# Splitting the normalised rows in the mixer and loading both parts in the feed-forward

## The chip, the cores and the metric

The kernel runs on one core of a Trainium2 chip. The metric is the time of one execution on the device in microseconds, as the median of several runs.

## The reference, cut to what matters

One encoder layer for 2048 tokens of width 1024: a gated token mixer, a normalisation, and a feed-forward with a convolution over three tokens.

```
x    = x + mixed @ w_out                      # the mixer's output
h2   = rms_norm(x, norm2_g)                   # (2048, 1024)
up   = depthwise_conv_seq(h2 @ w_up, conv_w, conv_b)     # w_up: 1024 x 5632
val, gate = split(up, 2)
x    = x + (silu(gate) * val) @ w_down        # w_down: 2816 x 1024
out  = rms_norm(x, final_g)
```

The tensor h2 of this reference, transposed, is what the change is about; the kernel calls it hT.

## The kernel before, in words

**Precision.** TensorE takes operands of the type fp32r. To keep fp32 accuracy the kernel splits each operand into a head (the value rounded to fp32r) and a tail (the value less its head, again in fp32r), and makes three products of the four: head-head, head-tail, tail-head (the list SPLIT). Every matmul group of the large products therefore comes in threes. Normally ScalarE or VectorE copies to get the head, and VectorE or GpSimd subtracts to get the tail.

**Phases.** Five functions run one after the other, each in a block of its own that all engines enter and leave together: the input projections, the Fourier branch, the attention, `mixer_output_phase` (L992) and `conv_ffn_phase` (L1303). They hand data on through scratch tensors in device memory. The change touches the last two. Tiles of the mixer are named mo_... in the profile, those of the feed-forward ff_....

**The mixer.** There are 4 token blocks b of 512 tokens (NBLK, BLK), each of 4 token tiles t of 128 (TPB). A block first has 8 stages s (L1257): 24 matmuls with the weight tile mix(s), which give 128 channels of both branches; VectorE gates and adds them (`gated`), and ScalarE and VectorE split the sum (`mix_heads`, `mix_tails`). Then each token tile is multiplied by w_out (`output`, L1272) in two halves of 24 matmuls. VectorE adds the residual half by half and normalises (`finish`), with ScalarE's `stats` between; TensorE transposes the normalised tile in 8 pieces of 128x128 into PSUM (`turn`, L1282); ScalarE copies these with the gain norm2_g as its scale into mo_turned and stores them to hT (`spill`, L1225 and L1228). `turn` and `spill` of a token tile n come one tile later; those of a block's last tile come at stage s = 1 of the next block, and the very last behind everything.

Each engine executes its own list strictly in order. In the mixer's stages the weights come through two raw buffers: SP loads a weight tile when the tail of the tile two before it is made, VectorE makes the head (`w_heads`, L1142), GpSimd the tail (`w_tails`, L1102), and TensorE waits for the tail. In the list of VectorE the call `w_heads(b, s, 2)` makes the heads of mix(s + 1) and out(s) ahead of `gated(b, s)`. In the output part VectorE also makes the heads of the next block's activations (`a_heads`, L1148), two for each token tile, and GpSimd their tails (L1107).

**The feed-forward.** The buffer h holds head and tail of the whole hT in SBUF. For each of 44 output tiles of 128 channels (`up`, L1644) TensorE runs 4 token blocks of 24 matmuls each, ScalarE takes out the result with the middle tap of the convolution (L1585), VectorE adds the side taps (L1490, L1493), and after each pair the product of both is stored. The second half of the phase multiplies by w_down (L1664).

At the start of the phase SP loads the weight tile 0, the 8 row blocks of hT of token block 0 into the 8 places of hraw, a small table, weight tile 1, and then the 24 row blocks of token blocks 1 to 3, each when its place in hraw is free (L1380). ScalarE makes the head of each (L1575), VectorE the tails of k = 0 to 5 (L1484) and GpSimd those of k = 6 and 7 (L1453). TensorE's tile 0 waits for the tail of each k of each block on its own.

Of the kernel before, what the change touches and what calls it, by code (L numbers as in the profile page):

```python
# [992 lines left out]
def mixer_output_phase(nc, x, fnT, atT, gT, w_mix, w_out, norm_g, eye, x2_out, hT_out):  # L993
# [7 lines left out]
    with ExitStack() as ctx:  # L1001
# [12 lines left out]
        turned_sb = m.sb("turned", [P, 1, KD, P])  # L1014
# [14 lines left out]
        turned, evac = m.sem("turned_mm"), m.sem("evac")  # L1029
# [91 lines left out]
        def _(dve):  # L1121
# [62 lines left out]

            w_heads(0, 0, 1)
            for k in range(KA):
                a_heads(0, k)
            for b in range(NBLK):
                for s in range(KD):
                    w_heads(b, s, 2 if s < KD - 1 or b < NBLK - 1 else 1)  # L1190
                    gated(b, s)
                    if s:
                        mix_tails(b * KD + s - 1)
                mix_tails(b * KD + KD - 1)
                for t in range(TPB):
                    finish(b, t)
                    if b < NBLK - 1:
                        a_heads(b + 1, 2 * t)
                        a_heads(b + 1, 2 * t + 1)

        @block.scalar
        def _(act):
# [40 lines left out]
            act.wait_ge(hT_stored, 16 * NTOK)  # L1243

        @block.tensor
        def _(pe):
# [52 lines left out]
def conv_ffn_phase(nc, x2, hT, w_up, w_down, conv, final_g, hid_d, out):  # L1299
# [6 lines left out]
    RING, RAW, HRAW = 3, 2, 8  # L1306
# [6 lines left out]
    with ExitStack() as ctx:  # L1313
# [7 lines left out]
        with ExitStack() as first:  # L1321
            hraw = Pool(nc, first, "ff").sb("hraw", [P, HRAW, BLK])
# [3 lines left out]
        with ExitStack() as first:  # L1326
# [9 lines left out]
        h_in, h_head, h_tail_dve, h_tail_pool = (  # L1336
            m.sems("h_in", HRAW), m.sem("h_head"), m.sem("h_tail_dve"), m.sem("h_tail_pool"))
# [10 lines left out]
        POOL_TAILS = (6, 7)  # L1348
        DVE_TAILS = tuple(k for k in range(KD) if k not in POOL_TAILS)

# [5 lines left out]

        def wait_h_tail(engine, b, k):
            if k in POOL_TAILS:
                engine.wait_ge(h_tail_pool, len(POOL_TAILS) * b + POOL_TAILS.index(k) + 1)
            else:  # L1360
                engine.wait_ge(h_tail_dve, len(DVE_TAILS) * b + DVE_TAILS.index(k) + 1)

# [3 lines left out]
        def _(sp):  # L1366
# [374 lines left out]
```

## Time and profile before

| | |
|---|---|
| runs | 3146.33 us median of 3 (3138.73 to 3149.79) |
| profiled execution | 3149.32 us, its span 3147.4 us |
| TensorE (PE) busy | 91% of the span |
| VectorE (DVE), ScalarE (ACT), GpSimd (POOL) busy | 38%, 22%, 22% |
| DMA | 349.22 MB, 111 GB/s over the span |
| mixer_output_phase | about 1180 to 1642 us |
| conv_ffn_phase, its start | first load at 1641.92 us |

In the rows below, times are in microseconds from the start of the span unless marked ns. A row of the timeline begins with the start and the duration of a run of like instructions; then come the engine, the line of the kernel, the operation, the destination and the sources with their shapes, the number of instructions, and in brackets the idle time of the engine before them and what ended it. PEld is TensorE's loading of weights, SPq and ACTq are the DMA issues of these engines. A row of the windows gives a stretch, its length, busy time and number of instructions of each engine, then the clock granted to TensorE as a share of full speed, the mean busy share of the 16 DMA engines, and what they moved.

### The profile page before, as it was taken

To read this page: it belongs to the slowest core of one execution; us is meant where nothing else is said; L and a number is where in the kernel's file an instruction comes from. 1 tells how busy PE (TensorE), PEld (TensorE's weight loads), DVE (VectorE), ACT (ScalarE), POOL (GpSimd) and SP (SyncE) were. 2 spreads that over 40 slices of the span, in tenths; PEclk is the share of its full clock that TensorE was granted. 3 is DMA by queue.
4 is the path that set the end of the run, shared out by engine and by line. 5 is a ranking of instruction groups with operands and counts; after the bars stand their busy time and mean duration, and the time that the engine had idled before them with its cause. 6 is when DMAs were issued, how large, how long until landed. Compare 5 with 4: busy or idle time off the path is not lost. (4 is left out here: it accounts for less than half of the span.)

```text
span 3147.4 us, 33077 instructions
## 1 busy us (share of the span) xinstructions
PE 2873.8 (91%) x13320; PEld 2361.9 (75%) x13320; DVE 1209.0 (38%) x1656; ACT 677.6 (22%) x1254; POOL 703.6 (22%) x293
## 2 busy tenths in 40 slices
PE   7999999993549996998879999999999998999998
PEld 6888888883548884776767888888888887888886
DVE  5200000004549885456534232323232323464564
ACT  4211111111236650211123111111111111111011
POOL 1010101012112315345412001100110011444442
PEclk9999999997769998999989999999999999999999
DMA  4321212113286736566643101110111013554543
GB/s 142 92 85 68 69 68 77 67 70 116 74 182 162 185 92 201 189 199 194 200 139 130 54 27 54 54 54 27 54 54 54 31 51 123 178 196 151 197 171 107
DMA packets 179704, 349.22 MB, mean 111 GB/s; under 512 B 59253, under 2 KB 80497, under 8 KB 173425
## 3 DMA queue, kind: packets, MB, share of 16 engines
q1 hardware_dynamic: 160624, 330.55, 32.9%
q10 hardware_dynamic: 18944, 16.78, 1.6%
q8 instruction: 95, 1.56, 0.2%
q14 instruction: 41, 0.33, 0.0%
HBM read 257.03 MB, written 91.78 MB: 111 GB/s over the span
## 5 line engine op out<-in xcount | busy, mean ns | idle before, releaser
L1644 PE MATMUL ff_psum<-ff_h,ff_w 128*128 128x512 f32 x4224 | 988.6, 395 | 17.7 <-DVE ff_h L1484 16.6
L1644 PEld LDWEIGHTS ff_psum<-ff_h,ff_w 128*128 128x128 f32 x4224 | 791.2, 187 | 215.1 <-POOL ff_w L1446 14.9
L1446 POOL TENSOR_TENSOR ff_w<-ff_wraw,ff_w 128x1024 fp32r<-128x1024 f32 x132 | 318.6, 2414 | 1190.3 <-DVE ff_w L1478 1190.3
L357 PE MATMUL in_psum<-in_hT,in_w 128*128 128x512 f32 x2304 | 522.6, 389 | 0.0
L357 PEld LDWEIGHTS in_psum<-in_hT,in_w 128*128 128x128 f32 x2304 | 432.6, 188 | 89.6
L1664 PE MATMUL ff_psum<-ff_w,ff_hid 128*128 128x512 f32 x2112 | 481.6, 391 | 9.3 <-DVE ff_hid L1502 9.1
L1664 PEld LDWEIGHTS ff_psum<-ff_w,ff_hid 128*128 128x128 f32 x2112 | 397.9, 188 | 92.9 <-issue 10.1
L1257 PE MATMUL mo_psum<-mo_act,mo_w 128*128 128x512 f32 x768 | 196.4, 412 | 59.4 <-POOL mo_w L1102 37.9
L1257 PEld LDWEIGHTS mo_psum<-mo_act,mo_w 128*128 128x128 f32 x768 | 147.9, 197 | 105.6 <-POOL mo_w L1102 47.9
L202 POOL TENSOR_TENSOR in_w<-in_wraw,in_w 128x1024 fp32r<-128x1024 f32 x32 | 77.1, 2413 | 620.4 <-DVE in_w L279 310.7
L1490 DVE SCALAR_TENSOR_TENSOR ff_gate<-ff_psum,ff_param,ff_gate 128x2047 f32<-128x2047 f32 x22 | 51.7, 2350 | 372.9 <-ACT ff_gate L1585 372.9
L348 PE MATMUL in_psum<-in_w,in_hT 128*128 128x512 f32 x768 | 180.9, 395 | 4.8 <-DVE in_hT L249 4.8
L1272 PE MATMUL mo_psum<-mo_wo,mo_mixed 128*128 128x512 f32 x768 | 178.2, 392 | 5.3 <-DVE mo_mixed L1164 5.3
L1478 DVE CAST ff_w<-ff_wraw 128x1024 fp32r<-128x1024 f32 x132 | 96.3, 730 | 217.6 <-PE ff_psum L1664 178.7
L348 PEld LDWEIGHTS in_psum<-in_w,in_hT 128*128 128x128 f32 x768 | 144.9, 190 | 35.0 <-DVE in_hT L249 5.2
L1272 PEld LDWEIGHTS mo_psum<-mo_wo,mo_mixed 128*128 128x128 f32 x768 | 143.2, 188 | 36.4 <-DVE mo_mixed L1164 7.3
L1585 ACT ACTIVATE ff_gate<-ff_psum,ff_param 128x512 f32<-128x512 f32 x88 | 68.5, 778 | 422.6 <-PE ff_psum L1644 422.6
L1490 DVE SCALAR_TENSOR_TENSOR ff_val<-ff_psum,ff_param,ff_val 128x2047 f32<-128x2047 f32 x22 | 51.7, 2350 | 271.5 <-ACT ff_val L1585 271.5
L1502 DVE TENSOR_TENSOR ff_hid<-ff_kraw,ff_hid 128x1024 fp32r<-128x1024 f32 x44 | 128.8, 2928 | 21.2 <-ACT ff_hid L1595 21.1
L960 PE MATMUL at_psum<-at_vs,at_pT 128*128 128x64 f32 x1024 | 134.5, 277 | 0.0
L276 DVE COPY in_bias_now<-in_gbias 128x1 f32 x16 | 2.5, 153 | 335.6 <-ACT in_stage L335 292.9
L960 PEld LDWEIGHTS at_psum<-at_vs,at_pT 128*128 128x128 f32 x1024 | 130.9, 201 | 0.0
(119 smaller groups left out, 2393.5 us busy)
## 6 DMA issues: line engine op xcount, KB each, us to landing
ff_wraw<-in_w_down_dram SPq DMA_DIRECT2D x88, 512.0 KB, 3.3
ff_wraw<-in_w_up_dram SPq DMA_DIRECT2D x44, 512.0 KB, 5.8
hidden<-ff_val SPq DMA_DIRECT2D x22, 1024.0 KB, 4.9
ff_kraw<-hidden SPq DMA_DIRECT2D x44, 512.0 KB, 4.5
at_bias<-shifted SPq DMA_DIRECT2D x72, 256.0 KB
in_wraw<-in_w_in_dram SPq DMA_DIRECT2D x32, 512.0 KB, 3.7
gT<-in_stage SPq DMA_DIRECT2D x64, 256.0 KB, 2.4
mo_wraw<-in_w_mix_dram SPq DMA_DIRECT2D x32, 512.0 KB, 3.8
```

Of the source, the lines that this page charges most:

```text
L202: nc.gpsimd.tensor_tensor(w[:, 1, s], wraw[:, t % RAW], f32(w[:, 0, s]), ALU.subtract).then_inc(w_tail, 1)
L348: last = nc.tensor.matmul(ps[:, bank(n)], hT[:, a, k, t * P:(t + 1) * P], w[:, b, 0:4, k], start=(k == 0 and (a, b) == SPLIT[0]), stop=(k ...
L357: last = nc.tensor.matmul(ps[:, bank], w[:, a, s, k], hT[:, c, k, b * BLK:(b + 1) * BLK], start=(k == 0 and (a, c) == SPLIT[0]), stop=(k = ...
L960: last = nc.tensor.matmul(ps[:, OB[n % 2], 0:HEAD_DIM], pT[:, n % 3, k], vs[:, h % 2, (ROW0[i] // 4 + k) * TJ + j], start=(k == 0), stop=( ...
L1257: last = nc.tensor.matmul(ps[:, 2 * (n % 2) + branch], w[:, a, s % 2, k], act_s[:, c, k], start=(k == ks[0] and (a, c) == SPLIT[0]), stop= ...
L1272: last = nc.tensor.matmul(ps[:, 4 + half], mixed[:, a, k, t * P:(t + 1) * P], wo[:, c, k, half * SPH:(half + 1) * SPH], start=(k == 0 and ...
L1446: nc.gpsimd.tensor_tensor(w[:, 1, n % RING], wraw[:, n % RAW], f32(w[:, 0, n % RING]), ALU.subtract).then_inc(w_tail, 1)
L1478: V.tensor_copy(w[:, 0, n % RING], wraw[:, n % RAW]).then_inc(w_head, 1)
L1490: V.scalar_tensor_tensor(out=dst[:, 1:SEQ], in0=row[:, 0:SEQ - 1], scalar=param[:, t, 0:1], in1=dst[:, 1:SEQ], op0=ALU.mult, op1=ALU.add). ...
L1502: V.tensor_tensor(hid[:, 1, n % 2], kraw[:, :, :], f32(hid[:, 0, n % 2]), ALU.subtract).then_inc(k_tail, 1)
L1644: last = nc.tensor.matmul(ps[:, 4 * (t % 2) + b], w[:, a, t % RING, k * P:(k + 1) * P], h[:, c, k, b * BLK:(b + 1) * BLK], start=(k == 0 a ...
L1664: last = nc.tensor.matmul(ps[:, 4 * half + i], hid[:, a, (b * PAIRS + pair) % 2, q, i * P:(i + 1) * P], w[:, c, n % RING, q * HALF:(q + 1) ...
```

## The change

In the mixer VectorE makes the tails of the transposed tile, too: PSUM value times gain, less the head. The tile mo_turned holds both parts. `spill` waits for the eight tails and stores both parts to hT, which gets a leading dimension of 2. In the feed-forward SP loads heads and tails straight to their places in h, with 64 loads of 256 KB in place of 32; hraw and the splitting of h go. The first token block waits for each k's two loads, the others for all 16 of their block. TensorE's `turn` waits for the tails where it waited for the heads.

```diff
@@ mixer_output_phase
-        turned_sb = m.sb("turned", [P, 1, KD, P])
+        turned_sb = m.sb("turned", [P, 2, KD, P], F32R)
@@ vector
+            def h_tails(n):
+                for k in range(KD):
+                    dve.wait_ge(h_head, KD * n + 4 * (k // 4) + 4)
+                    V.scalar_tensor_tensor(out=turned_sb[:, 1, k], in0=ps[:, 6 + k // 4, (k % 4) * P:(k % 4 + 1) * P],
+                                           scalar=gain[:, k:k + 1], in1=f32(turned_sb[:, 0, k]),
+                                           op0=ALU.mult, op1=ALU.subtract).then_inc(h_tail, 1)
...
                     gated(b, s)
                     if s:
                         mix_tails(b * KD + s - 1)
+                    if b and s == 1:
+                        h_tails(b * TPB - 1)
                 mix_tails(b * KD + KD - 1)
                 for t in range(TPB):
                     finish(b, t)
+                    if t:
+                        h_tails(b * TPB + t - 1)
                     if b < NBLK - 1:
                         a_heads(b + 1, 2 * t)
                         a_heads(b + 1, 2 * t + 1)
+            h_tails(NTOK - 1)
@@ scalar
             def spill(n):
                 act.wait_ge(turned, n + 1)
                 if n:
-                    act.wait_ge(hT_stored, 16 * n)
+                    act.wait_ge(hT_stored, 32 * n)
                 for k in range(KD):
                     nc.scalar.activation(turned_sb[:, 0, k], ps[:, 6 + k // 4, (k % 4) * P:(k % 4 + 1) * P], ACT.Copy,
-                                         scale=gain[:, k:k + 1]).then_inc(evac, 1)
-                act.wait_ge(evac, KD * (n + 1))
-                act.dma_start(hT_out.rearrange("(k p) t -> p k t", p=P)[:, :, n * P:(n + 1) * P],
-                              turned_sb[:, 0]).then_inc(hT_stored, 16)
+                                         scale=gain[:, k:k + 1]).then_inc(h_head, 1)
+                act.wait_ge(h_tail, KD * (n + 1))
+                for part in range(2):
+                    act.dma_start(hT_out[part].rearrange("(k p) t -> p k t", p=P)[:, :, n * P:(n + 1) * P],
+                                  f32(turned_sb[:, part])).then_inc(hT_stored, 16)
@@ tensor
             def turn(n):
                 pe.wait_ge(h2_done, n + 1)
-                at_least(pe, evac, KD * n)
+                at_least(pe, h_tail, KD * n)
@@ conv_ffn_phase, sync
             def load_h(b, k):
-                n = b * KD + k
-                if n >= HRAW:
-                    wait_h_tail(sp, b - 1, k)
-                sp.dma_start(hraw[:, k], hT[k * P:(k + 1) * P, b * BLK:(b + 1) * BLK]).then_inc(h_in[k], 16)
+                for part in range(2):
+                    sp.dma_start(f32(h[:, part, k, b * BLK:(b + 1) * BLK]),
+                                 hT[part, k * P:(k + 1) * P, b * BLK:(b + 1) * BLK]).then_inc(h_in[b + KD - 1 if b else k], 16)
@@ gpsimd, vector, scalar: h_tails and h_heads and the waits for them are gone
-            w_tails(0)
-            h_tails(0)
-            h_tails(1)
-            h_tails(2)
-            w_tails(1)
-            h_tails(3)
-            for n in range(2, TILES):
+            for n in range(TILES):
                 w_tails(n)
...
             w_heads(0)
-            for b in range(NBLK):
-                h_tails(b)
-                if b == 2:
-                    w_heads(1)
+            w_heads(1)
...
-            for b in range(NBLK):
-                for k in range(KD):
-                    h_heads(b, k)
             act.wait_ge(const_in, 16)
-            act.wait_ge(h_tail_pool, len(POOL_TAILS) * NBLK)
-            act.wait_ge(h_tail_dve, len(DVE_TAILS) * NBLK)
@@ tensor
                         if t == 0:
-                            wait_h_tail(pe, b, k)
+                            pe.wait_ge(h_in[b + KD - 1 if b else k], 32 * (KD if b else 1))
@@ encoder_layer
-    x2, hT = scratch("x2", SEQ, D), scratch("hT", D, SEQ)
+    x2, hT = scratch("x2", SEQ, D), scratch("hT", 2, D, SEQ)
```

## Rows read from the trace of the kernel before

**Rows 1.** Page, part 1: busy us, share of the span, instructions.

```profile
PE 2873.8 (91%) x13320; PEld 2361.9 (75%) x13320; DVE 1209.0 (38%) x1656; ACT 677.6 (22%) x1254; POOL 703.6 (22%) x293
```

**Rows 2.** Windows at the feed-forward's start, and one in the mixer's stages.

```profile
core 0: us, PE busy (x) PEld busy (x) DVE busy (x) ACT busy (x) POOL busy (x), PEclk, DMA share, GB/s
1642.00:1646.00 4.00, 0.00 (x0) 0.00 (x0) 0.50 (x1) 0.00 (x0) 0.00 (x0) 0.50 0.73 212
1646.00:1674.00 28.00, 21.99 (x84) 16.28 (x85) 20.82 (x26) 20.22 (x32) 13.90 (x9) 0.89 0.98 339
1650.00:1658.00 8.00, 8.00 (x31) 6.10 (x30) 4.54 (x8) 5.41 (x9) 2.58 (x2) 0.87 1.04 388
1644.00:1648.00 4.00, 0.00 (x0) 0.00 (x0) 0.69 (x1) 0.63 (x1) 1.73 (x1) 0.50 0.99 279
...
1556.00:1560.00 4.00, 4.00 (x12) 3.13 (x11) 3.97 (x5) 0.63 (x1) 2.38 (x1) 0.57 0.51 153
```

**Rows 3.** Timeline of the feed-forward's start.

```profile
1641.92 0.33 SPq L1374 DMA_DIRECT2D ff_wraw<-in_w_up_dram  x1
...
1646.27 2.34 POOL L1446 TENSOR_TENSOR ff_w<-ff_wraw,ff_w 128x1024 fp32r<-128x1024 f32 x1 [61.55 <-DVE ff_w L1478]
...
1649.31 11.53 PE L1644 MATMUL ff_psum<-ff_h,ff_w 128*128 128x512 f32 x42 [14.53 <-DVE ff_h L1484]
...
1673.22 0.63 ACT L1575 ACTIVATE ff_h<-ff_hraw 128x512 fp32r<-128x512 f32 x1 [0.15 <-DMA ff_hraw<-hT]
...
1675.54 44.83 PE L1644 MATMUL ff_psum<-ff_h,ff_w 128*128 128x512 f32 x191 [0.45 <-DVE ff_h L1484]
```

**Rows 4.** VectorE's groups by form: busy us, mean ns of one, idle before.

```profile
L583 DVE TENSOR_TENSOR ft_X<-ft_psum,ft_X 128x512 fp32r<-128x512 f32 x16 | 10.5, 686 | 11.7 <-ACT ft_X L628 11.7
...
L583 DVE TENSOR_TENSOR ft_X<-ft_psum,ft_X 128x256 fp32r<-128x256 f32 x4 | 1.7, 414 | 0.0
...
L594 DVE SCALAR_TENSOR_TENSOR ft_out<-ft_psum,ft_real 128x128 f32<-128x128 f32 x4 | 1.5, 380 | 0.0
```

**Rows 5.** Timeline from the end of mixer block 1 into block 2.

```profile
1418.10 2.15 ACT L1225 ACTIVATE mo_turned<-mo_psum,mo_gain 128x128 f32<-128x128 f32 x8
...
1419.11 0.75 DVE L1183 TENSOR_SCALAR mo_h<-mo_xt,mo_rstd 128x1024 f32<-128x1024 f32 x1
1419.78 0.76 DVE L1148 CAST mo_act<-mo_araw 128x512 fp32r<-128x512 f32 x2
...
1420.28 3.07 POOL L1107 TENSOR_TENSOR mo_act<-mo_araw,mo_act 128x512 fp32r<-128x512 f32 x2 [9.15 <-DVE mo_act L1148]
...
1423.31 2.81 POOL L1102 TENSOR_TENSOR mo_w<-mo_wraw,mo_w 128x1024 fp32r<-128x1024 f32 x1
...
1426.17 7.36 PE L1257 MATMUL mo_psum<-mo_act,mo_w 128*128 128x512 f32 x24 [1.80 <-POOL mo_w L1102]
...
1435.98 0.68 DVE L1164 TENSOR_TENSOR mo_mixed<-mo_mix,mo_mixed 128x512 fp32r<-128x512 f32 x1
...
1436.63 2.15 ACT L1225 ACTIVATE mo_turned<-mo_psum,mo_gain 128x128 f32<-128x128 f32 x8
1436.66 0.70 DVE L1142 CAST mo_w<-mo_wraw 128x1024 fp32r<-128x1024 f32 x1
...
1439.88 5.31 PEld L1257 LDWEIGHTS mo_psum<-mo_act,mo_w 128*128 128x128 f32 x24 [0.42 <-POOL mo_w L1102]
```

**Rows 6.** Timeline of the mixer's last token tiles.

```profile
1631.56 0.75 DVE L1183 TENSOR_SCALAR mo_h<-mo_xt,mo_rstd 128x1024 f32<-128x1024 f32 x1
1632.72 0.38 ACTq L1228 DMA_DIRECT2D hT<-mo_turned  x1
...
1636.01 2.17 ACT L1225 ACTIVATE mo_turned<-mo_psum,mo_gain 128x128 f32<-128x128 f32 x8 [3.32 <-DMA hT<-mo_turned]
1638.21 0.38 ACTq L1228 DMA_DIRECT2D hT<-mo_turned  x1
```

**Rows 7.** DMA view, 1632 to 1642 us: GB/s in 40 slices of 0.25 us.

```profile
GB/s 0 0 0 0 0 0 92 297 285 293 293 295 289 246 8 0 0 0 0 0 33 0 0 0 0 0 0 0 102 303 291 293 287 287 293 236 6 0 0 0
```

More of the change, by code:

```diff
@@ L1028, in mixer_output_phase @@
             m.sem(s) for s in ("out_mm", "x2_done", "sumsq_done", "mean_done", "root_done", "h2_done"))
-        turned, evac = m.sem("turned_mm"), m.sem("evac")
+        turned, h_head, h_tail = m.sem("turned_mm"), m.sem("h_head"), m.sem("h_tail")
         x2_stored, hT_stored = m.sems("x2_stored", 3), m.sem("hT_stored")
@@ L1242, in _ @@
                 act.wait_ge(x2_stored[s], 16 * len(range(s, NTOK, 3)))
-            act.wait_ge(hT_stored, 16 * NTOK)
+            act.wait_ge(hT_stored, 32 * NTOK)
         @block.tensor
@@ L1305, in conv_ffn_phase @@
     TILES = UP + NBLK * DOWN
-    RING, RAW, HRAW = 3, 2, 8
+    RING, RAW = 3, 2
     HALF = D // 2
@@ L1320, in conv_ffn_phase @@
         val0 = m.sb("val0", [P, SEQ])
-        with ExitStack() as first:
-            hraw = Pool(nc, first, "ff").sb("hraw", [P, HRAW, BLK])
         val1 = m.sb("val1", [P, SEQ])
@@ L1335, in conv_ffn_phase @@
         const_in, gain_in = m.sem("const_in"), m.sem("gain_in")
-        h_in, h_head, h_tail_dve, h_tail_pool = (
-            m.sems("h_in", HRAW), m.sem("h_head"), m.sem("h_tail_dve"), m.sem("h_tail_pool"))
+        h_in = m.sems("h_in", KD + NBLK - 1)
         w_in, w_head, w_tail, used = m.sems("w_in", RAW), m.sem("w_head"), m.sem("w_tail"), m.sem("used")
@@ L1345, in conv_ffn_phase @@
             m.sem(s) for s in ("added", "sumsq_done", "mean_done", "root_done", "step", "y_done", "stored"))
-        POOL_TAILS = (6, 7)
-        DVE_TAILS = tuple(k for k in range(KD) if k not in POOL_TAILS)
         def tile_done(engine, n):
@@ L1355, in tile_done @@
                 engine.wait_ge(up_mm, NBLK * (n + 1))
[L1357 to L1361, printed above, removed]
         block = ctx.enter_context(nc.Block())
@@ L1447, in w_tails @@
                                         ALU.subtract).then_inc(w_tail, 1)
-            def h_tails(b):
-                for k in POOL_TAILS:
-                    pool.wait_ge(h_head, b * KD + k + 1)
-                    at = slice(b * BLK, (b + 1) * BLK)
-                    nc.gpsimd.tensor_tensor(h[:, 1, k, at], hraw[:, k], f32(h[:, 0, k, at]),
-                                            ALU.subtract).then_inc(h_tail_pool, 1)
-            w_tails(0)
-            h_tails(0)
-            h_tails(1)
-            h_tails(2)
-            w_tails(1)
-            h_tails(3)
-            for n in range(2, TILES):
+            for n in range(TILES):
                 w_tails(n)
@@ L1478, in w_heads @@
                 V.tensor_copy(w[:, 0, n % RING], wraw[:, n % RAW]).then_inc(w_head, 1)
-            def h_tails(b):
-                for k in DVE_TAILS:
-                    dve.wait_ge(h_head, b * KD + k + 1)
-                    at = slice(b * BLK, (b + 1) * BLK)
-                    V.tensor_tensor(h[:, 1, k, at], hraw[:, k], f32(h[:, 0, k, at]), ALU.subtract).then_inc(h_tail_dve, 1)
             def sides(t):
@@ L1571, in _ @@
         def _(act):
-            def h_heads(b, k):
-                n = b * KD + k
-                act.wait_ge(h_in[k], 16 * (b + 1))
-                nc.scalar.activation(h[:, 0, k, b * BLK:(b + 1) * BLK], hraw[:, k], ACT.Copy).then_inc(h_head, 1)
             def centre(t, b):
```

## Prediction

> **What bounds the kernel now.** I read the page first, then the slices of the trace around the two functions that the change touches. TensorE is busy 2873.8 us of a span of 3147.4 [rows 1], so a change counts where TensorE stands still, or where it makes TensorE stand still. There are three such places: the start of the feed-forward, the seam between the functions, and the starts of the mixer's token blocks.
>
> At the start of the feed-forward the reader is to see the DMA engines, not ScalarE or VectorE. From 1646 to 1674 their busy share is 0.98 and they move 339 GB/s; in the best 8 us of it 388, in the 4 us around its start 279 [rows 2]. In that time the 32 raw blocks of hT arrive (8.39 MB), with weight tiles. The first matmul starts at 1649.31, when the first weight tile has its tail (GpSimd from 1646.27, 2.34 us), the last block has landed by 1673.22, where ScalarE takes it up, and from 1675.54 TensorE runs 191 matmuls in 44.83 us, 0.235 us each, without a stop [rows 3]. Nine of these belong to output tile 0 (96 matmuls in all, 87 came before, the first 42 of them in the row at 1649.31), so tile 0 ends at 1675.54 + 9 x 0.235 = 1677.7. The conversion in the feed-forward is therefore covered by a transfer that already fills the engines. After it TensorE is bound by itself.
>
> **The feed-forward's start, part by part.** Removed: 32 ScalarE copies, 24 VectorE and 8 GpSimd subtractions. Their cover was the transfer, so their removal is worth nothing but the lag from last landing to last matmul. Added: the loads are now 64 x 256 KB, 16.78 MB. Before the last one come weight tiles 0 and 1 and the table param (1.14 MB), 17.92 MB together; 4 us at 212 GB/s are 0.85 MB by 1646 [rows 2]. The other 17.07 MB take 50.4 us at 339 GB/s, so the last block lands at 1696.4 on the old time axis, 23.2 us later than 1673.2. Bounds: 44.0 us at 388 GB/s, 61.2 us at 279, so 16.8 to 34.0 us later. I take 339, the rate of the longest stretch of the same loads. SP's issues are not the limit: there are 32 more of about 0.5 us, 33 us in all for 64, beside 50.
>
> Blocks 1 to 3 each wait for all 16 of their pieces. So after the last landing all 24 matmuls of block 3 remain, 24 x 0.235 = 5.6 us, where before 1677.7 - 1673.2 = 4.5 us remained: 1.1 us more. TensorE also stands still about half of the time before: 4.19 MB at 339 GB/s are 12.4 us for a block with 5.6 us of matmuls. The clock falls after gaps: in 1556 to 1560, behind a gap at the weights, it was granted 0.57 and 12 matmuls ran in place of 17 [rows 2], 5 x 0.235 = 1.2 us. I put 1.5 us for block 3, between none and 5.6 us (all of it at 1.2 GHz in place of 2.4). Together **D = 23.2 + 1.1 + 1.5 = 25.8 us** (17.9 to 40.7). That SP asks for tile 2's weights only behind all 64 loads costs nothing: tile 1 was asked for before most of them and gives 22.5 us of matmuls. Late next is nothing that I see: the shift of tile 0 is the shift of the phase.
>
> The Trainium skill, "DMA: Bandwidth & Descriptors", § Bandwidth, gives 425 GB/s for a 16 MB load by one core alone and near 358 GB/s as a core's share of the memory. By 425 the 17.07 MB would take an estimated 40.2 us and D would be 15.6; by 358, 47.7 us and 23.1. The same page, § Issuing engines are not separate DMA queues, says that queues share the 16 engines, so neither splitting the issues nor moving them would help. The trace's 0.98 share at 339 speaks for the second figure, and the sum does not use either.
>
> **The tails in the mixer.** Added: 128 VectorE instructions of 128x128 from PSUM, eight for each of 16 token tiles. None such is in the trace. Nearest: a subtraction from PSUM of 512 columns takes 686 ns, of 256 columns 414, so 128 columns should take 278; a scalar_tensor_tensor of 128x128 from PSUM took 380 [rows 4]. I take 0.28 us, since the slope of the latter group (another line, with another output pattern) is steeper throughout: 8 x 0.28 = 2.2, with the switch-over 2.3 us a tile (up to 3.0). By the Trainium skill's "VectorE: DVE Perf Modes", § The TRN2 errata, an fp32 tensor_tensor takes (N + 151)/0.96 ns, an estimated 0.29 us here, which would change the sum by under 1 us.
>
> Twelve of the sixteen groups of tails stand right behind finish. Eight of these (t = 1 and 2) cost nothing: VectorE next waits for a 5.6 us half of output matmuls, and TensorE needs that half's sum only one half later. The one at t = 3 of block 3 belongs to the seam, below. At t = 3 of blocks 0 to 2 the next stage's start hangs on VectorE. In block 2: h2 is ready at 1419.87, the casts of the last two activations follow at once (1419.78 on the merged row), GpSimd makes their tails from 1420.28 to 1423.35 and then the weight tail of stage 1 from 1423.31, and TensorE, idle, starts stage 1 at 1426.17, as that ends [rows 5]. The tails of tile 4b+2 go between h2 and the casts; their heads are ready (ScalarE 1418.10 + 2.15). The chain moves by 2.3 us, and SP's next weight load, which waits for that tail, with it. **A = 3 x 2.3 = 6.9 us** (up to 9.1).
>
> The other three seams are at s = 1. VectorE ends mix_tails at 1436.66 and casts the weights of stage 3 at once; TensorE starts that stage behind their tail at 1439.88 [rows 5]. Now VectorE first does the tails of the last token tile of the block before. ScalarE makes their heads only from 1436.63, in 2.15 us; the first four tails start at about 1437.8 and end at 1438.9, the other four end at 1440.1. What queues behind them on VectorE is the cast, behind that GpSimd's tail, TensorE's stage 3 and SP's next load: 1440.1 - 1436.7 = 3.4 us. The load - cast - tail loop runs slower than TensorE to the end of the stages (the same loop lets TensorE stand still in most of them), so I let the delay stay. **B = 3 x 3.4 = 10.2 us** (up to 12.5).
>
> ScalarE's wait for the tails holds up stats(n+1) only, which comes some 9 us later. TensorE's wait for them in turn comes a token tile later. Both are covered, except at the end.
>
> **The seam.** Tile 15's h2 ends at 1632.31; the store of tile 14 was issued at 1632.72, landed by 1636.01, where ScalarE takes up the heads of tile 15, whose store goes out at 1638.21, and the feed-forward's first load at 1641.92, all of it one chain with TensorE idle [rows 3, 6]. Now the tails of tile 14 stand behind h2: 1632.31 + 2.24 = 1634.55, 1.8 us later than 1632.72. Two stores follow in place of one. A store of 0.52 MB moves at about 290 GB/s [rows 7], so the second adds 1.8 us to the landing. Behind the last heads come the last four tails, 4 x 0.28 + 0.1 = 1.2 us, and then again two stores, 1.8. **C = 1.8 + 1.8 + 1.2 + 1.8 = 6.6 us** (3.8 if a second store costs only its 0.38 us issue, 7.8 with tails of 0.38).
>
> **The sum.** A + B + C + D = 6.9 + 10.2 + 6.6 + 25.8 = 49.5 us on the profiled execution of 3149.3 us: 3198.8. The median of the runs is 3.0 us below that execution: **3195.8**.
>
> **Rivals.** First, the mixer's stages absorb the delays: if the load - cast - tail loop has slack, or VectorE catches up before stage 7, A and B vanish, and 3195.8 - 17.1 = 3178.7 is left. For it: the loop for the out weights waits mostly for DMAs. Against: TensorE starts stage 3 within 0.2 us of being free, behind a weight tail.
>
> Second, the doubled stream runs at its slowest rate, 279 GB/s, with TensorE's last block at 1.2 GHz: D = 40.7, and 3210.7. For it: the first 4 us of the loads ran so. Against: the 24 us after them were faster, with three engines at work on the same memory.
>
> Third, not slower: the start of the feed-forward hides the doubled transfer. Tile 0 took 28.4 us (1649.3 to 1677.7) for 22.5 us of matmuls, so 5.9 us could be won if conversion were what it waits for; with A and B absorbed and C = 6.6 the result would be 3147. It decides at the rate: the last block must land by 1672, which is 17.07 MB in 26 us, 657 GB/s. The trace's best is 388.
>
> **Chances.** Forecast 0.60, first rival 0.20, second 0.15, third 0.03, and 0.02 for a gain that I don't see. The range reaches from below the first rival to above the second: 3173 to 3213. A difference under 0.3% (9 us) can hardly be told from none: faster 0.01, same 0.03, slower 0.96.
>
> **What would show it.** In the profile after: (D) a DMA share near 1 for some 50 us from the feed-forward's start, three gaps of about 6 us in TensorE, and the uninterrupted run starting 25 us later in relation to the first matmul; (A, B) stage 1 of blocks 1 to 3 some 2.3 us later behind the last transpose, stage 3 a further 3.4; (C) some 6.6 us more from the last output matmul to the first load. It is wrong if the loads run over 400 GB/s or under 280, if the tails take over 0.4 us each, or if TensorE's idle time in the stages doesn't grow.

## The result, and the profile after

The changed kernel is slower: 3192.32 us median of 4 runs (3190.47 to 3196.40), against 3144.22 us for the kernel before in the same series, a ratio of 1.0155 with a 95% interval from 1.0133 to 1.0176. A second series on another occasion gave 3189.50 against 3147.02 us, 1.0144 (1.0127 to 1.0161); two slow runs of the kernel before in that series (3236.62 and 4553.74 us, at granted clocks of 0.883 and 0.600) are left out of the ratio. The prediction was 3195.8 us, 49.5 us over before; measured were 48.1 and 42.5 us.

The page of the profiled execution, parts 1 and 3 (for DMA queues: packets, megabytes, share of 16 engines):

```profile
span 3188.7 us, 33188 instructions
...
PE 2885.1 (90%) x13320; PEld 2373.9 (74%) x13320; DVE 1217.6 (38%) x1760; ACT 659.2 (21%) x1222; POOL 692.0 (22%) x285
...
q10 hardware_dynamic: 35584, 25.17, 2.5%
```

TensorE's work is what it was [rows 1]; VectorE has 104 instructions more (128 tails added, 24 removed). The whole moved 366.01 MB in place of 349.22: one more store of hT (q10 is ScalarE's queue) and one more load. Two executions also differ by chance: the mixer's first transpose came at 1281.38 us here and at 1285.19 before, 3.8 us earlier, for code that the change does not touch. So I read distances within each trace and not positions.

**The feed-forward's start.** Windows of the changed kernel, columns as in rows 2:

```profile
1664.00:1713.00 49.00, 26.35 (x74) 18.76 (x75) 1.39 (x2) 2.33 (x3) 4.68 (x2) 0.71 1.02 370
...
1684.00:1692.00 8.00, 1.13 (x3) 0.94 (x4) 0.00 (x0) 0.00 (x0) 0.00 (x0) 0.50 1.05 376
1692.00:1700.00 8.00, 7.10 (x23) 5.26 (x21) 0.00 (x0) 0.78 (x1) 0.00 (x0) 0.74 1.05 389
```

and its timeline, to be held against rows 3:

```profile
1660.15 0.33 SPq L1375 DMA_DIRECT2D ff_wraw<-in_w_up_dram  x1
...
1667.41 5.32 PE L1612 MATMUL ff_psum<-ff_h,ff_w 128*128 128x512 f32 x12 [19.26 <-POOL ff_w L1446]
1672.96 0.96 PE L1612 MATMUL ff_psum<-ff_h,ff_w 128*128 128x512 f32 x3 [0.24 <-DMA ff_h<-hT]
1675.81 3.93 PE L1612 MATMUL ff_psum<-ff_h,ff_w 128*128 128x512 f32 x9 [1.88 <-DMA ff_h<-hT]
1690.87 8.23 PE L1612 MATMUL ff_psum<-ff_h,ff_w 128*128 128x512 f32 x24 [11.13 <-DMA ff_h<-hT]
1701.69 7.39 PE L1612 MATMUL ff_psum<-ff_h,ff_w 128*128 128x512 f32 x24 [2.59 <-DMA ff_h<-hT]
1712.48 12.78 PE L1612 MATMUL ff_psum<-ff_h,ff_w 128*128 128x512 f32 x47 [3.40 <-DMA ff_h<-hT]
...
1719.93 0.78 ACT L1558 ACTIVATE ff_val<-ff_psum,ff_param 128x512 f32<-128x512 f32 x1 [10.03 <-PE ff_psum L1612]
```

The DMA engines are busy throughout (share 1.02) while VectorE, ScalarE and GpSimd do next to nothing. TensorE waits for the pieces of every block and runs the 24 matmuls of each of blocks 1 to 3 in 7.3 to 8.2 us in place of 5.6, at a lower clock behind the gaps (granted 0.50 in the row from 1684, most of which is a gap, and 0.71 over the stretch). The last block's wait ends 1712.48 - 1660.15 = 52.3 us behind the first load. ScalarE takes up tile 0's last sum at 59.8 us, and TensorE has begun tile 1 at 59.6; before, it did so at 35.8 (1677.7 - 1641.92). That is 23.8 us more. (The expectations below say 24.0, from 59.8 less 35.8, which are two different marks.)

**The seam.** Timeline of the changed kernel, to be held against rows 6:

```profile
1643.23 0.75 DVE L1183 TENSOR_SCALAR mo_h<-mo_xt,mo_rstd 128x1024 f32<-128x1024 f32 x1
1643.90 2.15 DVE L1188 SCALAR_TENSOR_TENSOR mo_turned<-mo_psum,mo_gain,mo_turned 128x128 fp32r<-128x128 f32 x8
1646.09 1.00 ACTq L1241 DMA_DIRECT2D hT<-mo_turned  x2
...
1651.23 2.17 ACT L1237 ACTIVATE mo_turned<-mo_psum,mo_gain 128x128 fp32r<-128x128 f32 x8 [6.61 <-DMA hT<-mo_turned]
1652.40 2.16 DVE L1188 SCALAR_TENSOR_TENSOR mo_turned<-mo_psum,mo_gain,mo_turned 128x128 fp32r<-128x128 f32 x8 [6.35 <-ACT mo_turned L1237]
1654.60 1.00 ACTq L1241 DMA_DIRECT2D hT<-mo_turned  x2
```

Four steps grew, each against its own in rows 6 and 3: from the end of h2 to the store of tile 14 2.1 us in place of 0.4; that store to the next heads 5.1 in place of 3.3; those heads to the store of tile 15 3.4 in place of 2.2; that store to the first load 5.6 in place of 3.7. Together 1.7 + 1.8 + 1.2 + 1.8 = 6.5 us.

**The mixer's blocks.** TensorE at the start of block 2 in the changed kernel (transposes are the 128x128 rows):

```profile
1416.79 1.03 PE L1295 MATMUL mo_psum<-mo_ident,mo_h 128*128 128x128 f32 x8
1417.58 4.34 PE L1270 MATMUL mo_psum<-mo_act,mo_w 128*128 128x512 f32 x18
1426.09 2.88 PE L1270 MATMUL mo_psum<-mo_act,mo_w 128*128 128x512 f32 x6 [4.17 <-POOL mo_act L1107]
1429.64 7.46 PE L1270 MATMUL mo_psum<-mo_act,mo_w 128*128 128x512 f32 x24 [0.67 <-POOL mo_w L1102]
1436.94 1.04 PE L1295 MATMUL mo_psum<-mo_ident,mo_h 128*128 128x128 f32 x8
1437.73 5.73 PE L1270 MATMUL mo_psum<-mo_act,mo_w 128*128 128x512 f32 x24
1446.95 12.80 PE L1270 MATMUL mo_psum<-mo_act,mo_w 128*128 128x512 f32 x48 [3.49 <-POOL mo_w L1102]
```

The same place in the kernel before, where the last row holds stages 2 and 3:

```profile
1415.69 1.03 PE L1282 MATMUL mo_psum<-mo_ident,mo_h 128*128 128x128 f32 x8
...
1434.15 11.46 PE L1257 MATMUL mo_psum<-mo_act,mo_w 128*128 128x512 f32 x48
```

Stage 1 starts 12.85 us behind the transpose at 1416.79; before, it was 1426.17 [rows 5] behind the transpose at 1415.69, 10.48 us. Stage 3 starts 9.2 us behind stage 2 (1446.95 less 1437.73) in place of 5.7 (1439.88 less 1434.15). What stands in between on VectorE and GpSimd:

```profile
1440.18 2.15 ACT L1237 ACTIVATE mo_turned<-mo_psum,mo_gain 128x128 fp32r<-128x128 f32 x8
1441.33 2.16 DVE L1188 SCALAR_TENSOR_TENSOR mo_turned<-mo_psum,mo_gain,mo_turned 128x128 fp32r<-128x128 f32 x8 [1.13 <-ACT mo_turned L1237]
1443.41 0.69 DVE L1142 CAST mo_w<-mo_wraw 128x1024 fp32r<-128x1024 f32 x1
...
1444.17 2.72 POOL L1102 TENSOR_TENSOR mo_w<-mo_wraw,mo_w 128x1024 fp32r<-128x1024 f32 x1 [5.12 <-DVE mo_w L1142]
```

The tails wait for their heads, the cast of stage 3's weights waits for the tails, and GpSimd for the cast: the chain of the prediction. A measure for all three blocks is the time from the mixer's first transpose to its last but one. The first two rows are the kernel before, the last two the changed one:

```profile
1285.19 1.03 PE L1282 MATMUL mo_psum<-mo_ident,mo_h 128*128 128x128 f32 x8
...
1628.14 1.03 PE L1282 MATMUL mo_psum<-mo_ident,mo_h 128*128 128x128 f32 x8
```

```profile
1281.38 1.04 PE L1295 MATMUL mo_psum<-mo_ident,mo_h 128*128 128x128 f32 x8
...
1639.82 1.03 PE L1295 MATMUL mo_psum<-mo_ident,mo_h 128*128 128x128 f32 x8
```

342.9 us and 358.4 us, 15.5 us more. With 6.5 and 23.8 that makes 45.8 us, between the two measured differences.

The windows of just these stretches say in what form TensorE spends the 15.5 us (before, then changed):

```profile
1285.19:1628.14 342.95, 309.79 (x1361) 248.27 (x1360) 184.11 (x277) 63.01 (x178) 144.83 (x69) 0.98 0.58 186
```

```profile
1281.38:1639.82 358.44, 317.75 (x1362) 254.79 (x1360) 209.67 (x389) 63.07 (x178) 146.70 (x69) 0.95 0.62 198
```

It idles 40.7 us in place of 33.2, and it is at work 317.7 us in place of 309.8 on the same matmuls, at a granted clock of 0.95 in place of 0.98. Over the four profiled executions with the mixer of before, idle is 31.2 to 34.7 and work 309.0 to 313.3; over the five with the changed mixer they are 40.7 to 44.0 and 313.1 to 317.7. So the waits are the larger part on average, and behind them the matmuls run slower: stage 3 of blocks 1 and 3 took 8.55 us in place of 5.73. How much of this a later wait would have filled anyway is not shown.

Three distances, in us, will do for all kernels below. "Blocks" is the one just read, "seam" goes from the last transpose but one to the feed-forward's first load, "start" from there to ScalarE's first take-out of output tile 1 (which follows tile 0 by its first block). Where the code of a stretch is the same, "blocks" differs by up to 1.9 us from one execution to another (342.9 to 344.8 with the mixer of before), "start" by up to 1.7 (41.6 to 43.3 with the feed-forward of before), "seam" by 0.1.

| kernel | blocks | seam | start | ratio to before (95% interval) |
|---|---|---|---|---|
| before | 342.9 | 13.8 | 41.6 | |
| changed | 358.4 | 20.3 | 65.4 | 1.0155 (1.0133 to 1.0176) |
| changed, again | 358.2 | 20.4 | 65.6 | 1.0144 (1.0127 to 1.0161) |
| mixer's part alone | 357.8 | 20.4 | 41.6 | 1.0058 (1.0045 to 1.0072) |
| feed-forward's part alone | 344.6 | 13.8 | 66.1 | 1.0067 (1.0054 to 1.0080) |
| one part loaded, no splitting | 344.8 | 13.8 | 43.1 | 1.0000 (0.9991 to 1.0008) |
| stores alone | 347.3 | 17.8 | 43.3 | 1.0017 (1.0006 to 1.0027) |
| tails alone | 358.0 | 16.6 | 42.2 | 1.0046 (1.0033 to 1.0059) |
| changed, tails moved | 354.1 | 20.4 | 65.3 | 1.0110 (1.0096 to 1.0125) |
| changed, early store | 356.9 | 17.8 | 63.9 | 1.0134 (1.0116 to 1.0153) |
| changed, two tiles | 358.2 | 20.4 | see below | 1.0091 (1.0074 to 1.0107) |
| changed, finer waits | 357.0 | 20.4 | 59.4 | 1.0114 (1.0098 to 1.0131) |
| changed, all four | 349.2 | 17.8 | see below | 1.0039 (1.0026 to 1.0052) |
| before, two tiles | 343.6 | 13.8 | see below | 0.9983 (0.9974 to 0.9991) |

### The profile page after: what moved, and what is told of

Same layout as the page of the kernel before. It is cut to its first block and busy times, and to the rows that moved or that the text cites. A ratio compares the mean times of both kernels' runs of the same rounds, so it can differ in the third digit from the quotient of the medians.

```text
span 3188.7 us, 33188 instructions
## 1 busy us (share of the span) xinstructions
PE 2885.1 (90%) x13320; PEld 2373.9 (74%) x13320; DVE 1217.6 (38%) x1760; ACT 659.2 (21%) x1222; POOL 692.0 (22%) x285
## 2 busy tenths in 40 slices
DMA packets 200952, 366.01 MB, mean 115 GB/s; under 512 B 60020, under 2 KB 97648, under 8 KB 194672
## 5 line engine op out<-in xcount | busy, mean ns | idle before, releaser
L1612 PEld LDWEIGHTS ff_psum<-ff_h,ff_w 128*128 128x128 f32 x4224 | 800.9, 190 | 234.0 <-DMA ff_h<-hT 22.8
L1270 PE MATMUL mo_psum<-mo_act,mo_w 128*128 128x512 f32 x768 | 204.2, 426 | 67.8 <-POOL mo_w L1102 38.2
L1270 PEld LDWEIGHTS mo_psum<-mo_act,mo_w 128*128 128x128 f32 x768 | 154.5, 206 | 115.3 <-POOL mo_w L1102 47.9
L348 PEld LDWEIGHTS in_psum<-in_w,in_hT 128*128 128x128 f32 x768 | 144.5, 190 | 34.7 <-DVE in_hT L249 5.2
L1558 ACT ACTIVATE ff_val<-ff_psum,ff_param 128x512 f32<-128x512 f32 x88 | 68.1, 773 | 330.5 <-PE ff_psum L1612 330.5
```

Source lines behind the costliest of these rows:

```text
L348: last = nc.tensor.matmul(ps[:, bank(n)], hT[:, a, k, t * P:(t + 1) * P], w[:, b, 0:4, k], start=(k == 0 and (a, b) == SPLIT[0]), stop=(k ...
L1270: last = nc.tensor.matmul(ps[:, 2 * (n % 2) + branch], w[:, a, s % 2, k], act_s[:, c, k], start=(k == ks[0] and (a, c) == SPLIT[0]), stop= ...
L1558: nc.scalar.activation(dst[:, b * BLK:(b + 1) * BLK], ps[:, 4 * (t % 2) + b], ACT.Identity, scale=param[:, t, 1:2], bias=param[:, t, 3:4]) ...
L1612: last = nc.tensor.matmul(ps[:, 4 * (t % 2) + b], w[:, a, t % RING, k * P:(k + 1) * P], h[:, c, k, b * BLK:(b + 1) * BLK], start=(k == 0 a ...
```

## The experiments

**Each half alone.** The first kernel has the changed mixer and the feed-forward of before:

```diff
-                sp.dma_start(hraw[:, k], hT[k * P:(k + 1) * P, b * BLK:(b + 1) * BLK]).then_inc(h_in[k], 16)
+                sp.dma_start(hraw[:, k], hT[0, k * P:(k + 1) * P, b * BLK:(b + 1) * BLK]).then_inc(h_in[k], 16)
```

> The mixer of the changed kernel with the feed-forward of before: the mixer makes and stores both parts, the feed-forward loads the first part as its raw rows and splits them, so the tails of hT are left out of the products. Measures A + B + C alone. The theory of the prediction: about 22 us over before (17 in the mixer's blocks 1 to 3, 6.6 at the seam); read from the trace of the changed kernel 15.5 + 6.6 = 22. Rival (the delays in the stages are an accident of one execution, or come from the doubled transfer behind them): under 10 us. The distance from the last transpose but one to the feed-forward's first load: 20.3 us here, 13.8 before. From that load on the phase is as before.

The second has the mixer of before and the changed feed-forward:

```diff
-                                 hT[part, k * P:(k + 1) * P, b * BLK:(b + 1) * BLK]).then_inc(h_in[b + KD - 1 if b else k], 16)
+                                 hT[k * P:(k + 1) * P, b * BLK:(b + 1) * BLK]).then_inc(h_in[b + KD - 1 if b else k], 16)
```

> The mixer of before with the feed-forward of the changed kernel: both parts are loaded from the raw rows, so the second part holds the rows again in place of their tails. Measures D alone, the doubled transfer without the splitting. The theory: 24 us over before (24.0 in the changed kernel's trace from the first load to the last sum of output tile 0), mixer and seam as before. If A to D are independent, the two halves add up to the whole, 46 to 48 us. Rival (the start of the feed-forward suffers from the mixer's later end, its clock or its stores in flight): D alone well under 24.

Measured: 1.0058 and 1.0067. By the ratios that is 18 and 21 us, by the medians 22.0 and 22.4 (3169.43 and 3169.90 against 3147.47). Each half shows its own distances and leaves the others as before: 357.8 and 20.4 with a start of 41.6; 344.6 and 13.8 with a start of 66.1. The halves together give 39 us by the ratios, where the whole, measured twice, gives 49 and 45; by the medians 44.4, against 48.1 and 42.5. By the trace the halves add up (14.9 + 6.6 + 24.5 = 46.0), so I take them as independent; with intervals of some 4 us to either side on each half and 5 to 7 on the whole, the runs don't speak against it, and nothing that only both together cost shows in a row.

**What the removed splitting was worth.** The feed-forward half again, with one part in place of two:

```diff
-                for part in range(2):
+                for part in range(1):
                     sp.dma_start(f32(h[:, part, k, b * BLK:(b + 1) * BLK]),
...
-                                                    h[:, c, k, b * BLK:(b + 1) * BLK],
+                                                    h[:, 0, k, b * BLK:(b + 1) * BLK],
```

> As the one before, with one part loaded in place of two (8.39 MB as in the kernel before, but straight into place and without splitting); the matmuls read the first part in place of the second, so the tails of hT are left out of the products, their number is the same. Measures what the removed splitting is worth alone. The theory (the transfer binds, the splitting was covered): the last block lands as before, some 31 us after the first load, then 24 matmuls: tile 0 ends 1 to 3 us later than before, the whole is within 3 us of before. Rival (conversion was what tile 0 waited for): 5.9 us faster than before. Against the run with both parts: some 22 us less, which is 8.39 MB at 370 GB/s, if bytes set the time.

Measured 1.0000: the 64 instructions that the change takes off three engines are worth nothing that can be measured. The start is 1.5 us later, no more than it varies with the feed-forward of before. Both parts against one: 66.1 - 43.1 = 23.0 us for 8.39 MB, 365 GB/s. The trace adds a point that I had not put so:

```profile
1648.18 8.11 PE L1599 MATMUL ff_psum<-ff_h,ff_w 128*128 128x512 f32 x24 [15.08 <-POOL ff_w L1433]
1659.86 100.50 PE L1599 MATMUL ff_psum<-ff_h,ff_w 128*128 128x512 f32 x423 [3.57 <-DMA ff_h<-hT]
```

With one part TensorE waits once, 3.57 us for block 1, and never again. One part keeps up with TensorE from there (2.1 MB per 5.6 us of matmuls are 375 GB/s, about what the engines move), two parts cannot. The kernel before, which loads as many bytes, stands near this edge too.

**More work for each block.** If D is TensorE waiting with too little to do, another order helps:

```diff
-            for t in range(UP):
-                up(t)
+            for b in range(NBLK):
+                up(0, [b])
+                up(1, [b])
+            for t in range(2, UP):
+                up(t, range(NBLK))
```

> The changed kernel with another order of TensorE's first two output tiles in the feed-forward: block by block, each for tile 0 and tile 1, in place of tile by tile. All eight banks of PSUM are in use for it as before. Each block now brings 11.2 us of matmuls for some 11.3 us of its transfer. The theory (D is a transfer that TensorE waits for with too little work at hand): the end of tiles 0 and 1 moves from 82.3 us behind the first load (59.8 + 22.5) to about 52.3 + 11.3 + 1 = 65 us, 17 us less than the changed kernel, and the clock no longer falls between the blocks. Rival (D comes from the traffic itself, as slower matmuls, weights or stores): under 5 us of gain.

```profile
1651.94 0.33 SPq L1377 DMA_DIRECT2D ff_wraw<-in_w_up_dram  x1
...
1670.98 1.64 PE L1614 MATMUL ff_psum<-ff_h,ff_w 128*128 128x512 f32 x3 [1.92 <-DMA ff_h<-hT]
1675.70 64.52 PE L1614 MATMUL ff_psum<-ff_h,ff_w 128*128 128x512 f32 x263 [3.08 <-POOL ff_w L1448]
```

From 1675.70 TensorE runs without a stop. 168 of the 192 matmuls of both tiles remain there and take 42.1 us (39.4 at full clock; granted were 0.81 in the first 14 us and 0.93 over the whole), so tile 2 starts 65.9 us behind the first load, in place of 82.0 in the changed kernel. That is 16 us less. In the runs: 1.0091 against 1.0144, 17 us by the ratios and 16 by the medians, as expected, though the engines still move 369 GB/s at a share of 1.03 in the 48 us from 1656. So the cost was TensorE waiting with too little to do, not the traffic as such. What stops TensorE last is now the tail of weight tile 1 (3.08 us, GpSimd).

**Finer waits.** Blocks 1 to 3 wait for pairs of k:

```diff
-                            pe.wait_ge(h_in[b + KD - 1 if b else k], 32 * (KD if b else 1))
+                            pe.wait_ge(h_in[KD + 4 * (b - 1) + k // 2 if b else k], 32 * (2 if b else 1))
```

> The changed kernel with finer waits in the feed-forward: blocks 1 to 3 wait for each pair of k on its own (four semaphores a block) in place of all 16 pieces. The theory: after the last landing only 6 of 24 matmuls remain, and TensorE works a little all the time; tile 0 ends 2 to 3 us behind the last landing in place of 7.4, so 4 to 5 us less than the changed kernel. Rival (the coarse waits cost nothing, since the clock and not the count of matmuls sets the lag): under 2 us.

The start is 59.4 us in place of 65.4, and the ratio 1.0114 in place of 1.0144, an interval that overlaps (1.0098 to 1.0131 against 1.0127 to 1.0161) with the middle 9 us lower; the medians are 6 us apart. The rows show how:

```profile
1707.01 1.67 PE L1612 MATMUL ff_psum<-ff_h,ff_w 128*128 128x512 f32 x6 [1.05 <-DMA ff_h<-hT]
1709.68 30.60 PE L1612 MATMUL ff_psum<-ff_h,ff_w 128*128 128x512 f32 x130 [1.00 <-DMA ff_h<-hT]
```

A pair comes each 2.7 us (1.05 MB, 388 GB/s), with 1.66 us of matmuls and a gap of 1.05 us, and in gaps so short the clock stayed up (granted 1.00 from 1685 to 1713): six matmuls take 1.66 us, where 24 behind a gap of 11.1 us took 8.2. The start is 6.0 us earlier, so of the lag of 7.3 us behind the last landing about 6 were the coarse wait and its clock.

**The seam.** The first part is stored before the tails are made:

```diff
-                act.wait_ge(h_tail, KD * (n + 1))
-                for part in range(2):
+                for part, ready in enumerate((h_head, h_tail)):
+                    act.wait_ge(ready, KD * (n + 1))
```

> The changed kernel, but spill stores the first part as soon as the heads are made and waits for the tails only then, for the second part. The theory of the seam (C = waits for tails, then two stores one behind the other, twice): the first store moves while the tails are made, the second one's landing then hangs on the tails and one store's 3.3 us: some 1.7 us less at the store of tile 14 and 1.2 at that of tile 15. From the last transpose but one to the first load 17.4 us in place of 20.3 (13.8 before); in total 2.9 us less than the changed kernel. Rival (each issue on ScalarE or the landing costs a fixed time, not the queueing of the bytes): no change.

The seam is 17.8 us in place of 20.3, 2.6 less where 2.9 were expected. The ratio, 1.0134 against 1.0144, can't show so little. Blocks and start came out 1.5 us shorter each, within what they vary by.

**Moving the tails.** Here an expectation failed:

```diff
                     w_heads(b, s, 2 if s < KD - 1 or b < NBLK - 1 else 1)
+                    if b and s == 0:
+                        h_tails(b * TPB - 2)
+                    if b and s == 2:
+                        h_tails(b * TPB - 1)
                     gated(b, s)
...
-                    if b and s == 1:
-                        h_tails(b * TPB - 1)
...
-                    if t:
+                    if t and (t < TPB - 1 or b == NBLK - 1):
                         h_tails(b * TPB + t - 1)
```

> The changed kernel with two of the calls for tails moved in VectorE's list: those of a block's third tile from ahead of the casts of the last activations to behind the weight casts of stage 0, those of its last tile from stage 1 to behind the weight casts of stage 2. Nothing else differs. The theory (VectorE's order makes A and B): stage 1 of blocks 1 to 3 again 10.5 us behind the last transpose (12.9 in the changed kernel), stage 3 again 5.7 to 7.3 us behind stage 2 (9.2 to 10.9), and some 15 us less than the changed kernel, so some 31 to 33 us over before. Rival (the doubled stores delay the weights, whatever the order): no change in those distances and 46 to 48 us over before.

```profile
1300.33 1.03 PE L1297 MATMUL mo_psum<-mo_ident,mo_h 128*128 128x128 f32 x8
...
1310.79 7.68 PE L1272 MATMUL mo_psum<-mo_act,mo_w 128*128 128x512 f32 x24 [1.19 <-POOL mo_w L1102]
...
1319.11 5.73 PE L1272 MATMUL mo_psum<-mo_act,mo_w 128*128 128x512 f32 x24
1326.37 5.73 PE L1272 MATMUL mo_psum<-mo_act,mo_w 128*128 128x512 f32 x24 [1.54 <-POOL mo_w L1102]
1334.54 7.37 PE L1272 MATMUL mo_psum<-mo_act,mo_w 128*128 128x512 f32 x24 [2.43 <-POOL mo_w L1102]
```

Both marks are back: stage 1 stands 10.46 us behind the transpose, stage 3 7.3 us behind stage 2. But the blocks took 354.1 us, only 4.3 less than changed, not 15. Stage 2 now comes 8.3 us behind stage 1 (6.5 before), stage 4 8.2 behind stage 3 (7.7 before), stage 5 8.4 behind stage 4 (7.2 before): the delay moved on. The runs, 1.0110 or 35 us over before, look nearer to the 31 to 33 expected, but the three distances add up to 41.4 us over before; in the profiled execution the mixer's first transpose came 8.4 us earlier than before, in code that the change doesn't touch. I go by the distances. Two kernels took the cause apart. One stores twice and makes no tails:

```diff
-                for k in range(KD):
-                    dve.wait_ge(h_head, KD * n + 4 * (k // 4) + 4)
-                    V.scalar_tensor_tensor(out=turned_sb[:, 1, k], in0=ps[:, 6 + k // 4, (k % 4) * P:(k % 4 + 1) * P],
-                                           scalar=gain[:, k:k + 1], in1=f32(turned_sb[:, 0, k]),
-                                           op0=ALU.mult, op1=ALU.subtract).then_inc(h_tail, 1)
+                pass
...
-                                  f32(turned_sb[:, part])).then_inc(hT_stored, 16)
+                                  f32(turned_sb[:, 0])).then_inc(hT_stored, 16)
```

> Open since the run with the tails moved: A + B was to vanish there, but from the first transpose to the last but one the mixer took 354.1 us, against 342.9 before and 358.4 in the changed kernel. This kernel is the mixer of the changed kernel without the 128 tails of VectorE: the first part is stored twice, the feed-forward of before loads it once, so the tails of hT are left out of the products. Theory V (VectorE's tails make the delay, and moving them only shifts it within the stages, where VectorE has no free 2 us): 343 us here, and 17.4 us from the last transpose but one to the first load (two stores twice, 13.8 + 2 x 1.8). Theory S (the doubled stores hold up the weights in the stages): 347 to 354 us here.

The other makes the tails and stores once:

```diff
-                for part in range(2):
+                for part in range(1):
                     act.dma_start(hT_out[part].rearrange("(k p) t -> p k t", p=P)[:, :, n * P:(n + 1) * P],
```

> The counterpart: the mixer of the changed kernel with the tails, but only the first part stored, and the feed-forward of before, so again the tails of hT are left out of the products. Theory V: 357 to 358 us from the first transpose to the last but one, as with both; theory S: 347 to 354. At the seam what the tails alone add, 1.7 + 1.2: 16.7 us. The two seams together, 3.6 + 2.9, should give the 6.5 us of the changed kernel.

Transposes, first and last but one: of the stores alone, then of the tails alone.

```profile
1285.92 1.04 PE L1291 MATMUL mo_psum<-mo_ident,mo_h 128*128 128x128 f32 x8
...
1633.18 1.04 PE L1291 MATMUL mo_psum<-mo_ident,mo_h 128*128 128x128 f32 x8
```

```profile
1284.94 1.03 PE L1295 MATMUL mo_psum<-mo_ident,mo_h 128*128 128x128 f32 x8
...
1642.92 1.04 PE L1295 MATMUL mo_psum<-mo_ident,mo_h 128*128 128x128 f32 x8
```

347.3 and 358.0 us. The tails alone cost all of it (15.1 of 15.5 us): theory V. But the stores alone cost 4.4 us too (2.5 against the slowest execution of the mixer of before), at the edge of what S asked for; with the tails beside them they cost 0.4, no more than chance. That may explain a part of the failed expectation: with the tails out of the way the stores can come out (4.4 of the 11.2 us that remained over before).

What the other 6.8 us are stays open. Two things in the trace of the moved tails bear on it. First, over its blocks TensorE is at work 316.2 us (309.8 before) and idle 37.8 (33.2 before): of the 11.2 us only 4.6 are waits, the rest is matmuls at a lower clock, granted 0.96.

```profile
1276.74:1630.81 354.07, 316.23 (x1361) 252.60 (x1360) 210.74 (x389) 63.19 (x178) 143.37 (x69) 0.96 0.63 201
```

Stage 1 in the rows above is an example. Its matmuls took 7.68 us, those of the same stage before 5.74, and stage 2 follows them and the transposes without a wait. The mixer of before shows such slow stages too, in other blocks and executions, so a part of this can be chance, and why the clock fell here is not shown. Second, VectorE is not short of time in that stage, where it is busy 4.1 of 8.3 us. It stands idle for the landing of a weight:

```profile
1318.54 0.69 DVE L1142 CAST mo_wo<-mo_wraw 128x1024 fp32r<-128x1024 f32 x1 [2.90 <-DMA mo_wraw<-in_w_out_dram]
```

So "VectorE has no free 2 us", which the expectation of the stores alone supposed, does not hold for that stage. It may for later ones: in stage 4 of block 1 before, VectorE is busy 5.5 of 7.2 us.

At the seam the two add, 4.0 for the stores and 2.9 for the tails, 6.8 against 6.5 together.

**All four together.** Tails moved, early store, finer waits, two tiles block by block:

> The changed kernel with the four variants together: tails moved, first part stored early, finer waits, first two tiles block by block. Can the change be made to pay? Theory: 44 us over before, less 4 in the stages, less 2.6 at the seam, less 17 at the start of the feed-forward, where the finer waits find nothing more: 18 to 21 us over before. If it still loses, splitting in the mixer costs more than it can give back, whatever the order, since the last landing 52 us behind the first load stays.

Measured 1.0039 (1.0026 to 1.0052), 12 us over before and less than I expected. The trace says 16: 6.3 in the blocks, 4.0 at the seam, and tile 2 starts 64.0 us behind the first load in place of 58.2. The blocks took 349.2 us, 5 less than with the tails moved alone; TensorE idles 34.6 us in them, about as before, and is at work 314.7. The early store alone took off 1.5 us there; that it does more beside moved tails is a guess that no run separates. The change in this order, the best one that I ran, still loses.

**Two tiles in the kernel before.** The same order of TensorE, on the old kernel, with the splitting of weight tile 1 pulled forward:

```diff
             for b in range(NBLK):
                 h_tails(b)
-                if b == 2:
+                if b == 0:
                     w_heads(1)
```

> The kernel before, not the changed one, with TensorE's first two output tiles block by block, and the head and tail of weight tile 1 made right behind those of block 0. The theory (tile 0 took 28.4 us for 22.5 us of matmuls, the rest is waiting for blocks): both tiles end some 54 us behind the first load in place of 58.3, so 4 to 5 us less than before, a ratio of 0.9985. Rival (the conversion of hT and of weight tile 1 then stand in each other's way): no gain or a loss of 1 to 2 us.

```profile
1647.88 8.32 PE L1646 MATMUL ff_psum<-ff_h,ff_w 128*128 128x512 f32 x24 [15.38 <-DVE ff_h L1486]
1656.65 63.63 PE L1646 MATMUL ff_psum<-ff_h,ff_w 128*128 128x512 f32 x270 [0.44 <-POOL ff_w L1448]
```

The first load was at 1640.51, so both tiles end at 1656.65 + 39.4 = 1696.1, 55.6 us behind it in place of 58.3. The ratio is 0.9983 (0.9974 to 0.9991), 3 to 8 us faster than before: of all kernels here the only one whose interval lies below 1. The rows account for the 2.7 us at the start; 4 to 5 were expected.

## Why the prediction was right, step by step

- *Transfers bind the feed-forward's start.* Right. The rate was 370 GB/s where 339 had been taken, so the last wait ended 21.0 us later (52.3 less 31.3), not 23.2. SP's issues took 41.2 us for the 64 loads where 33 had been estimated, but the last went out 9.4 us before the last wait ended, so they did not bind. Of the rows of before, that of 388 was nearer. That the stream ran faster because its loads no longer wait for places in hraw is my reading; no run shows it by itself. Of the Trainium skill's two figures in "DMA: Bandwidth & Descriptors", § Bandwidth, 358 GB/s as a core's share was passed here and 425 for 16 MB was not reached, with the load at 2 KB a row.
- *1.1 us for the coarse wait and 1.5 for the clock.* The lag behind the last wait was 7.3 us in place of 4.5, 2.8 more; 2.6 was the sum of the two. The gaps came out otherwise than said: one of 11.1 us and two of 2.6 and 3.4, not three of 6. Block 0 waits for each k on its own, so its matmuls ran while its own pieces landed, and the gap behind it is the whole transfer of block 1. The waits for blocks 2 and 3 each end 10.8 us after the one before, and matmuls at the lower clock fill 8.2 and 7.4 us of that. D: 25.8 predicted, 23.8 measured.
- *The removed splitting is worth nothing.* Right, by the run with one part (1.0000).
- *A = 3 x 2.3.* Right: stage 1 stands 12.84, 12.85 and 12.85 us behind the last transpose, 10.46 to 10.48 before, 2.4 us each. Eight tails took 2.15 us, where 2.2 were taken. The 0.28 us of the forecast was right as the time from one start to the next (0.27), not as the duration of one (343 ns); the estimate by the Trainium skill's "VectorE: DVE Perf Modes", § The TRN2 errata, 0.29 us, fits neither the duration nor the step exactly and lies between.
- *B = 3 x 3.4.* Right at its place, 3.55, 3.5 and 4.75 us, but not all of it stayed: over the blocks the two terms came to 4.9, 6.5 and 4.1 us, together 15.5, where 17.1 had been predicted. At their places the two make 18.9 us, so 3.4 were won back: in blocks 1 and 3 stage 5 followed stage 4 in 5.5 and 5.6 us, 7.2 and 7.4 before. The statement that the delay stays to the end of the stages was right in kind and too strong by these 3.4; that A and B were put 1.8 too low at their places hid half of it, which is luck. Left out were the slower clock behind the waits (8.0 us more at work in this execution) and the doubled stores beside the weights, which cost 4.4 us alone and 0.4 here.
- *C = 6.6.* Right, term by term: 1.7, 1.8, 1.2, 1.8 us.
- *The sum.* 49.5 predicted, 45.8 by the distances, 48.1 and 42.5 by the medians. D was 2.0 too high, A and B together 1.6; that the first series lies within 1.4 us of the forecast is chance.
- The rivals fell: the stages absorbed little of the delay, the stream was not at its slowest, and a transfer of 17 MB was not hidden.

## What to carry to other kernels

Splitting data at its producer doubles the bytes of the store and of the load; it can pay only where the consumer's split is on its critical path and the transfer is not, and here it was the other way round. Before moving work off a phase, see what covers it: here a DMA share near 1 over the same stretch went with no gain from 64 instructions less (1.0000) and 23 us lost for 8.39 MB more. Where a phase must start on a stream, try more work for each piece (two output tiles a block, 16 us here) and waits for small pieces (6 us). When waits move or grow, look at the time at work, too, and not only at the idle time: the clock can fall behind them.

## What the runs showed of the hardware

- One core's loads of 256 KB, 2 KB a row, ran at 370 GB/s over 49 us and at 389 in the best 8 us shown (changed kernel).
- Stores with rows of 512 B moved at about 290 GB/s; a second one behind the first added 1.8 us of landing each time.
- TensorE lost 1.6 to 2.6 us for a block of 24 matmuls behind gaps of 2.6 to 11.1 us (changed kernel). Behind gaps of 1.05 us that came every 2.7 us the granted clock was 1.00 and 6 matmuls took 1.66 us (finer waits).
